# Expert matmuls in plain fp32 on four 32-column tiles of TensorE, without the hi/lo split of weights and activations

## The reference, cut to what matters

```python
def expert_choice_ffn(h, w_router, w_gate_up, w_down):
    B, N, D = h.shape
    cap = CAP_FACTOR * N // N_EXPERTS            # 64 sample tokens, 16 prompt tokens
    aff = jax.nn.softmax((h @ w_router).astype(jnp.float32), axis=-1)
    g, idx = lax.top_k(jnp.swapaxes(aff, 1, 2), cap)
    xs = jax.vmap(lambda hb, ib: hb[ib])(h, idx)
    gu = jnp.einsum('becd,edf->becf', xs, w_gate_up)      # 1024 -> 2 x 1024
    gate, up = jnp.split(gu, 2, axis=-1)
    y = jnp.einsum('becf,efd->becd', jax.nn.silu(gate) * up, w_down) * g[..., None]
    return jax.vmap(lambda ib, yb: jnp.zeros((N, D), yb.dtype).at[ib.reshape(-1)].add(yb.reshape(-1, D)))(idx, y)
```

## Time and profile before

| | us |
|---|---|
| median of 3 runs (927.48 to 930.04) | 929.23 |
| span of the profiled execution | 926.3 |
| expert matmuls, first start to the first matmul of the last stage | 350.5 to 901.4 |
| last stage | 901.4 to 926.3 |

### The profile page before, as it was taken

The page is one execution under the profiler, slowest core; times in us unless marked ns, Lnnn a source line. Parts: engine busy times, 40 slices in busy tenths (PEclk is TensorE's granted clock), DMA queues, the critical chain, the costliest instruction groups (busy, mean ns, idle before and its releaser), DMA issues.

```text
span 926.3 us, 12681 instructions
## 1 busy us (share of the span) xinstructions
PE 880.6 (95%) x5127; PEld 625.9 (68%) x5127; DVE 775.7 (84%) x828; ACT 583.5 (63%) x606; POOL 159.5 (17%) x109
## 2 busy tenths in 40 slices
PE   6989999698899979999999999999999999999995
PEld 5779977466688865666666666666666666666663
DVE  4579654889789877898998998898998998898877
ACT  2365376756622236777777777777777777777752
POOL 0000300010011052002312311321320320320220
PEclk9999999999999988999999999999999999999998
DMA  9920540450086479999999999999999999999717
GB/s 338 389 92 6 206 183 1 183 183 2 4 319 255 185 317 363 379 416 389 402 403 389 388 412 391 388 415 385 385 416 381 377 414 381 382 401 391 253 14 204
DMA packets 59349, 272.80 MB, mean 294 GB/s; under 512 B 6728, under 2 KB 7036, under 8 KB 42908
## 3 DMA queue, kind: packets, MB, share of 16 engines
q1 hardware_dynamic: 50848, 245.33, 67.3%
q0 software_dynamic: 7536, 24.00, 9.2%
q10 hardware_dynamic: 908, 2.68, 0.8%
HBM read 257.99 MB, written 14.00 MB: 294 GB/s over the span
## 4 chain that ended last, share of the span: by engine, by line
PE 81%; DVE 8%; ACT 5%; DMA 3%; issue 2%; SPq 1%; ACTq 0%; DVEq 0%
PE PS L998 23%; PE PS L999 23%; PE PS L1000 23%; PE PS L1213 2%; PE PS L1197 2%; DMA w_qkv<-in_w_in 2%; PE PS L1236 1%; PE PS L1375 1%; PE PS L1388 1%; PE PS L1167 1%; DMA acc_scratch<-ysc,idx_u 1%; ACT WX L726 1%; ACT xnT L669 1%; PE PS L1021 1%; PE PS L1289 1%
## 5 line engine op out<-in xcount | busy, mean ns | idle before, releaser
L1927 DVE TENSOR_TENSOR Wl<-wr,Wh 128x2048 fp32r<-128x2048 f32 x190 | 432.6, 2290 | 52.2 <-ACT Wh L912 52.1
L912 ACT ACTIVATE Wh<-wr 128x2048 fp32r<-128x2048 f32 x192 | 367.4, 1915 | 69.6 <-PE PS L1000 69.5
L998 PE MATMUL PS<-Wh,Xh 128*80 128x512 f32 x512 | 203.3, 397 | 1.3 <-ACT gate_act L934 0.8
L1000 PE MATMUL PS<-Wl,Xh 128*80 128x512 f32 x512 | 201.9, 394 | 0.0
L999 PE MATMUL PS<-Wh,Xl 128*80 128x512 f32 x512 | 201.7, 394 | 0.0
L564 POOL DMA_INDIRECT acc_scratch<-ysc,idx_u x15 | 81.2, 5412 | 418.5 <-DVE ysc L1958 418.5
L1000 PEld LDWEIGHTS PS<-Wl,Xh 128*80 128x80 f32 x512 | 76.1, 149 | 42.5 <-issue 0.7
L998 PEld LDWEIGHTS PS<-Wh,Xh 128*80 128x80 f32 x512 | 76.2, 149 | 42.1 <-issue 1.9
L999 PEld LDWEIGHTS PS<-Wh,Xl 128*80 128x80 f32 x512 | 76.2, 149 | 39.7 <-issue 0.7
L998 PE MATMUL PS<-Wh,HTh 128*80 128x512 f32 x256 | 101.6, 397 | 0.0
L999 PE MATMUL PS<-Wh,HTl 128*80 128x512 f32 x256 | 100.4, 392 | 0.0
(11 more groups left out here) (314 smaller groups left out, 1226.3 us busy)
## 6 DMA issues: line engine op xcount, KB each, us to landing
wr<-in_w_gate_up SPq DMA_DIRECT2D x128, 1024.0 KB, 12.2
wr<-in_w_down SPq DMA_DIRECT2D x64, 1024.0 KB, 11.0
ring<-in_w_mod SPq DMA_DIRECT2D x24, 1024.0 KB, 10.2
ring<-in_w_in SPq DMA_DIRECT2D x4, 1024.0 KB, 11.4
ring<-in_w_out SPq DMA_DIRECT2D x4, 1024.0 KB, 6.6
w_qkv<-in_w_in SPq DMA_DIRECT2D x4, 768.0 KB, 14.1
h_scratch<-h POOLq DMA_DIRECT2D x5, 512.0 KB, 5.5
acc_scratch<-xt POOLq DMA_DIRECT2D x5, 512.0 KB, 5.9
```

Of the source, the lines that this page charges most:

```text
L912: act.activation(Wh[n % NWH][:], wr[s][:], ACT.Copy).then_inc(W_hi, 1)
L998: pe.matmul(out, w[0], x[0], start=first, stop=False)
L1000: return pe.matmul(out, w[0], x[1], start=False, stop=last)
L1927: dve.tensor_tensor(Wl[s][:], wr[s][:], Wh[n % NWH][:].bitcast(F32), ALU.subtract).then_inc(W_lo, 1)
```

## The change

The expert matmuls take the weights as they land, in fp32, and the activations unsplit. The stationary operand is cut into 32 columns: the 64 sample columns make two tiles, the 16 prompt columns with 16 zeros one. In gate/up each slot has three groups of four matmuls of 512 columns: sample rows of gate (two row tiles by two column halves), sample rows of up, and prompt rows of all four quarters. A down slot has two groups for the samples and one for the prompt, in which the four tiles are two f blocks by two halves; the two f blocks are added on ScalarE and VectorE (`odd_half`, `y_prompt_rows`). So 12 matmuls per slot remain, in plain fp32, and results lie on 128 partitions. The split copies are gone, the space of `Wh` becomes three more slots (16 in all). `x_transposes` is one call after k = 3 and `h_transposes` one call two slots after the last gate/up slot; the latter transposes four 128x128 blocks of samples and four 48-row blocks of the prompt. GpSimd clears the padding columns instead of splitting two slots.

```diff
-NSLOT, NWH = 13, 4
+NSLOT, N_LOW = 16, 13
-X_AT, H_AT = (1, 4), (2, 3)
+X_AT, H_AT = 3, 2
@@ GpSimd
-        for n in range(W_POOL):
-            pool.wait_ge(W_hi, n + 1)
-            pool.tensor_tensor(Wl[n][:], wr[n][:], Wh[n][:].bitcast(F32), ALU.subtract).then_inc(W_lo, 1)
+        pool.wait_ge(lg_ps, CH)
+        for buf in (XT[0], XT[1], HT[0], HT[1]):
+            pool.memset(buf[:, :, SL:SLQ], 0.0).then_inc(zeroed, 1)
@@ ScalarE
+        def odd_half(e):
+            act.wait_ge(W_used, DN_END[e] + 1)
+            if e:
+                act.wait_ge(y_ok, e)
+            b = dn_banks(e)[1]
+            for a in range(2):
+                act.activation(y_odd[CAP_S:SL, H2 * a:H2 * a + H2], PS[64 + 32 * a:64 + 32 * a + CAP_P, 512 * b:512 * b + 512],
+                               ACT.Copy, scale=g_slot[CAP_S:SL, e:e + 1]).then_inc(odd_ok, 1)
...
-        act.activation(yh[0][:], ysc[0][:], ACT.Copy).then_inc(yh_ok, 1)
+        act.wait_ge(W_used, len(ORDER) - 4)
+        act.activation(yh[0][0:CAP_S, :], ysc[0][0:CAP_S, :], ACT.Copy).then_inc(yh_ok, 1)
         for h in range(2):
             act.wait_ge(y_ok, NE + h)
-            act.activation(yh[1][:, 512 * h:512 * h + 512], ysc[1][:, 512 * h:512 * h + 512], ACT.Copy).then_inc(yh_ok, 1)
+            act.activation(yh[1][0:CAP_S, H2 * h:H2 * h + H2], ysc[1][0:CAP_S, H2 * h:H2 * h + H2], ACT.Copy).then_inc(yh_ok, 1)
+        odd_half(NE - 1)
+        act.wait_ge(y_ok, NE + 2)
+        act.activation(yh[1][CAP_S:SL, :], ysc[1][CAP_S:SL, :], ACT.Copy).then_inc(yh_ok, 1)
@@ TensorE, gate/up slot
-                for q in range(4):
-                    cs = slice(512 * q, 512 * q + 512)
-                    last = three(bank(q, rows=SL), x, (Wh[hs][:, cs], Wl[s][:, cs]), k == 0, k == KC - 1)
+                for b, lo in ((GATE_B, 0), (UP_B, 1024)):
+                    for j in range(4):
+                        pe.matmul(PS[32 * j:32 * j + 32, 512 * b:512 * b + 512], x[:, 32 * (j % 2):32 * (j % 2) + 32],
+                                  w[:, lo + 512 * (j // 2):lo + 512 * (j // 2) + 512], start=(k == 0), stop=(k == KC - 1))
+                for j in range(4):
+                    last = pe.matmul(PS[32 * j:32 * j + 32, 512 * GU_P_B:512 * GU_P_B + 512], x[:, CAP_S:SLQ],
+                                     w[:, 512 * j:512 * j + 512], start=(k == 0), stop=(k == KC - 1))
@@ VectorE
+        def y_prompt_rows(e):
+            b = dn_banks(e)[1]
+            for a in range(2):
+                dve.wait_ge(odd_ok, 2 * e + a + 1)
+                last = dve.scalar_tensor_tensor(y_sum[CAP_S:SL, H2 * a:H2 * a + H2], PS[32 * a:32 * a + CAP_P, 512 * b:512 * b + 512],
+                                                g_slot[CAP_S:SL, e:e + 1], y_odd[CAP_S:SL, H2 * a:H2 * a + H2], ALU.mult, ALU.add)
+            link(last)
+            return dve.tensor_tensor(ysc[e % 2][CAP_S:SL, :], y_sum[CAP_S:SL, :], G2[CAP_S:SL, :], ALU.mult)
@@ y_evac
+            if e < NE - 1:
+                y_sample_half(e, 0)
+                y_sample_half(e, 1)
+                y_prompt_rows(e).then_inc(y_ok, 1)
@@ VectorE, last stage
         y_lo(1, 0, 0, H2)
         y_lo(1, 1, H2, D)
+        y_prompt_rows(NE - 1).then_inc(y_ok, 1)
+        dve.wait_ge(yh_ok, 4)
+        dve.tensor_tensor(yl[1][CAP_S:SL, :], ysc[1][CAP_S:SL, :], yh[1][CAP_S:SL, :].bitcast(F32), ALU.subtract).then_inc(yl_ok, 1)
         for c in range(FIN_ADD):
```

More of the change, by code:

```diff
@@ L100 @@
 OUT_ORDER = (PC,) + tuple(range(PC))
-W_POOL = 2
 N_HOLD = 8
@@ L903, in _, with x_copy @@
         act.activation(aff[:, 0:PC, :], aff[:, 0:PC, :], ACT.Exp).then_inc(lexp_ok, 1)
[L906 to L924, removed]
+        def x_copy(e):
+            act.wait_ge(x_t, 2 * e + 1)
+            act.activation(XT[e % 2][:, 0:4, 0:SL], x_bank(0).rearrange("p (k s) -> p k s", k=4), ACT.Copy).then_inc(xT_s[0], 1)
         def silu_gate(e):
@@ L948, in _ @@
+        x_copy(0)
+        for n in range(len(ORDER)):
             for e in range(NE):
[L949 to L952, removed]
+                if n == GU_END[e]:
                     silu_gate(e)
-                for h in range(2):
-                    if n == GU_END[e] + H_AT[h] + LEAD:
-                        h_split(e, h)
+                if e + 1 < NE and n == GU0[e] + X_AT:
+                    x_copy(e + 1)
+                if n == GU_END[e] + H_AT:
+                    hT_copy(e)
+                if n == DN_END[e] and e < NE - 1:
+                    odd_half(e)
@@ new lines, in _ @@
+                for j in range(4):
+                    last = pe.matmul(PS[32 * j:32 * j + 32, 512 * GU_P_B:512 * GU_P_B + 512], x[:, CAP_S:SLQ],
+                                     w[:, 512 * j:512 * j + 512], start=(k == 0), stop=(k == KC - 1))
+            else:
+                bs, bp = dn_banks(e)
+                if k == 0:
+                    pe.wait_ge(hTs_ok, e + 1)
+                    pe.wait_ge(hTp_ok, e + 1)
+                    if e and e < NE - 1:
+                        pe.wait_ge(y_ok, e)
+                for f in (2 * k, 2 * k + 1):
+                    lo = 1024 * (f % 2)
+                    for j in range(4):
+                        pe.matmul(PS[32 * j:32 * j + 32, 512 * bs:512 * bs + 512],
+                                  HT[e % 2][:, f, 32 * (j % 2):32 * (j % 2) + 32],
+                                  w[:, lo + 512 * (j // 2):lo + 512 * (j // 2) + 512], start=(f == 0), stop=(f == KC - 1))
+                for j in range(4):
+                    f, lo = 2 * k + j // 2, 1024 * (j // 2) + 512 * (j % 2)
+                    last = pe.matmul(PS[32 * j:32 * j + 32, 512 * bp:512 * bp + 512], HT[e % 2][:, f, CAP_S:SLQ],
+                                     w[:, lo:lo + 512], start=(k == 0), stop=(k == KC // 2 - 1))
@@ L1435, in _ @@
+            last.then_inc(W_used, 1)
+            if kind == "gu" and e + 1 < NE and k == X_AT:
+                x_transposes(e + 1)
+            for e_ in range(NE):
+                if n == GU_END[e_] + H_AT:
+                    h_transposes(e_)
         pe.wait_ge(y_ok, NE - 1)
```

259 lines of the change are left out of this document (120 added, 139 removed).

## The result

| | median us | lowest to highest | ratio to the kernel before, 95% interval |
|---|---|---|---|
| before, same chip | 929.63 | 927.48 to 931.61 (4 runs) | |
| after | 912.42 | 911.85 to 913.64 (4 runs) | 0.9823 [0.9802, 0.9843] |

17.2 us less, 1.8%, well outside the 0.3% that can be told from no change. The profiled execution of after took 912.27 us with a span of 910.5, against the span of 926.3 in the earlier trace rows: 15.8 us less.

The account below looks back on a forecast made before the run. TensorE was taken to bound the experts, 6 us behind the weights' floor. Its end 22.8 us earlier and a tail 4.0 us longer made -18.8, so 929.2 - 18.8 = 910.4 us; range 900 to 925.

Parts of the forecast that it names:

- one round of four tiles: Expert matmuls: four records, one per tile, take 0.43 us; 1152 rounds make 495.4 us.
- transposes and 31 changes of form: Experts on TensorE: transposes 23.3 us; 31 excursions from four tiles to the full array and back, 0.23 each, 7.1 us.
- first rounds at the lower clock: Start of the experts: TensorE's first matmuls run at the lower clock and cost 2.3 us more.
- wait before expert 1's gate and up: Not priced; the wait examined was `h_transposes` for silu and two products, some 2 us, with two slots, 5.2 us, for it.
- tail: After W, the last `W_used`: chunk 0's statistics start at W + 8.0 instead of W + 3.2; net +4.0 us, bounds +1 to +7.
- start of the stage: First expert matmul: stays where it was, since 8 slots lie ready and the first rows' copies end as early.
- Rival C: Expert matmuls: rounds do not overlap and are 0.592 us apart, +187 us, 1097; chance 0.06.
- rival D: Expert matmuls: the form does not hold the full clock; at 1.2 GHz +495 us, 1405; chance 0.04.
- the other bound, 37 us: Changes of form on TensorE: upper bound, 0.6 us, a whole record, each way; the lower bound was 0 if later ones hide.
- The weights' floor: Experts: the last weights land at about 870, plus one slot 873; TensorE was expected to end 6 us behind it.
- Rival A: Experts: the weights become the bound, stage end 873, 904.8 us, or 902 with the tail at +1; chance 0.10.
- Splits hidden: Experts: ScalarE and VectorE lose 367 and 433 us of splits, priced at nothing since they were not on the path.

Follow-up runs that it names:

- the second profile of before: The kernel before, unchanged, run and profiled once more: 929.86 us, ratio 0.9996, span 928.5, experts from 352.82 to 903.92.
- four variants: The changed kernel with 13 slots (911.15 us), without the prompt tail (907.98), with a new prompt tail (908.42), or with VectorE kept busy (913.08).
- with VectorE kept busy: Against the changed kernel, two extra VectorE products of 128x512 on a scratch tile in every slot: 913.08 us, ratio 0.9822.
- The two kernels with the waits per bank: The changed kernel with waits per bank before gate/up: 911.85 us; with the new prompt tail and chunk 0 loaded from ScalarE's queue as well: 906.28 us.
- the runs with less work: Against the changed kernel with 13 slots, the prompt group of four matmuls left out in all slots but the first of each matrix: 909.68 us, ratio 0.9793.
- the second profile of after: The changed kernel, unchanged, run and profiled once more: 912.31 us, ratio 0.9816, span 909.4, stage 351.80 to 880.56.
- the one without VectorE's last two: Against the changed kernel, expert 15's prompt product with G2 on GpSimd, its rows added by plain fp32 matmuls without `yh` and `yl`: 908.42 us, ratio 0.9777.

## Why the prediction was right

912.42 us against 910.4, within the range; the ledger in spans was -18.8 and came to -15.8, or -18.0 against the second profile of before (928.5 - 910.5), whose experts start as late as those of after. Term by term:

| term | predicted | measured |
|---|---|---|
| one round of four tiles | 0.43 us | 0.43 (slot 2.58) |
| transposes and 31 changes of form | 23.3 + 7.1 = 30.4 | 15 x 0.81 + 16 x 1.07 = 29.3 |
| first rounds at the lower clock | 2.3 | 4.07 - 2.57 = 1.5 |
| wait before expert 1's gate and up | none | 2.4 (before 0.9) |
| stage in all | 528.1 | 528.7, 528.8; in four variants 529.8 to 530.1 (before 550.9, 551.1) |
| tail | +4.0 | +3.9 (28.8 for 24.9) |
| start of the stage | 0 | +2.5 by this pair of profiles, +0.2 by the other |

That the stage comes out only 0.6 us off is luck in part: the missed wait of 2.4 us is set off by 1.1 too much for transposes and changes of form and 0.8 too much for the low clock.

**The round** was read from 256-column rows and doubled, and held for 1152 rounds. Rival C falls with it. The rule quoted there from the Trainium skill ("TensorE: Matmul & The Clock Gate", Part 3), 3.07x for four row tiles, is not what this form of four column tiles shows: untiled records are 0.429 apart and rounds of four 0.43, four for the price of one. Why the page's figure is lower can't be told from here, since row tiles were not run.

**The clock** (rival D) was granted in full, 1.00 from 385 to 880. After the wait before expert 1 it fell in five of the nine profiles of changed kernels that have this wait, though not in the two of after itself; the stage of the kernels with 13 slots, without the prompt tail and with VectorE kept busy was then 530.0 to 530.1 us. Why it fell in some and not in others stays open.

**The changes of form** were read from single gaps of 0.09 and 0.13 to 0.14; an added one costs 0.26 to 0.27. The word "hidden", 0 us, and the other bound, 37 us, are both far off.

**The wait at 378.43** is the step that failed. I looked for a wait at `h_transposes`, which has two slots of time; the silu of expert 0 is also what the gate and up banks of expert 1 wait for, and there the order of the slots puts no down products between. The other experts have them, and it costs once: 375.14 + 0.86 = 376.00, next matmul 378.43. It stood in a row of before, in the timeline and among the waits of that stage, which the prediction passed over with "waits for almost nothing":

```profile
376.51 0.43 PE L998 MATMUL PS<-Wh,Xh 128*80 128x512 f32 x1 [0.78 <-ACT gate_act L934]
```

With the interval of 0.23 before it, that is 0.9 us of idle time. The old kernel waited there bank by bank (`if e == 1 and k == 0`), and the change put one wait for all banks in its place. The two kernels with the waits per bank bring it back to 1.0.

**The weights' floor** I put at 873 and found at 877 (matmuls of the last stage at 876.7 when TensorE is no bound). In that execution the experts began at 352.26, 1.7 us later than in the earlier trace rows. And I took the median landing of the earlier trace rows, 5.1 us, for the last slot, where the longest was 7.3: in the first profile of before the DMAs still move 354 GB/s from 871 to 872 us and 23 in the next. The two make 3.9 us, against 3.7 missing (4.6 by the last slot's start). Rival A did not occur in after, but it is near: 1.5 us of full clock at the start and 1.4 from the bank waits were enough to make TensorE wait for weights. A faster TensorE would have gained some 4 us at most and, by the runs with less work and with the bank waits, little of it at the end, since chunk 1 of `xf` is used at 886.00 and 884.89 there and at 886.39 in after.

**The tail** went as worked out step by step: statistics at W + 8.1 for W + 8.0. That the scatter goes out at W - 3.7 and not at W - 5.8 is the load of chunk 0 behind the weights, landing later than my 872. This differs between executions: in the second profile of after it is W - 4.6, and with 13 slots and in the two kernels with the tail changed it waits for VectorE and goes out at W - 5.7, as predicted. In after it cost an idle 0.63 us on TensorE and nothing on VectorE's chain. The kernel without the prompt steps and the one without VectorE's last two give 4.3 and 3.9 us back, the whole term: it was VectorE's chain alone that set the end. I had doubted my own term there and was wrong to.

**Splits hidden.** VectorE gave up 351 us of work from 385 to 880 (449.35 there before, 97.99 after) and ScalarE 310 (364.43 and 54.13); the kernel without splits or tiles is 127 us slower. Freeing the two engines was worth nothing by itself, as TensorE sets the pace in all these kernels.

## What to carry to other kernels

Count TensorE's columns in the new form before counting what other engines save: a plain fp32 matmul of 512 columns is two records of 0.43 us, against 0.229 for an fp32r one and 0.69 for three of them; it pays here only because the short stationary operands leave room for four tiles, and only if successive matmuls go to different tiles. When the bounding stage is shortened, look at what is now just behind it, here a weight queue some 4 us away over the stage, and less at one point, and a load queued behind the weights, because it takes the next gain. Steps of few rows cost their columns, so in a tail that one engine sets, 16 rows are as dear as 80 and are worth moving to an idle engine even at twice the time.

## What the runs showed of the hardware

- Matmuls on four 32-column tiles issued tile after tile run 2.7 at a time over the stage, not one and not four (0.160 us per record against 0.107 in turn and 0.429 in order).
- 1.99 us of idle TensorE in the tail was followed by 5 us at 0.50 of the clock (1.2 GHz), and four matmuls took 3.78 us instead of 1.98; 0.63 us of idle time in the kernel after was not. The length of the idle time alone does not decide it: some 2.4 us before expert 1 were followed by a lower clock in five profiles (0.57 from 376 to 380 us with 13 slots) and by the full clock in four, the two of after among them.
- An excursion from 128x32 tiles to the full array and back costs 0.26 to 0.27 us.
- GpSimd's indirect scatter took 5.44 us to issue beside VectorE products of 2.29 us each, 1.44 without, and 1.74 beside products of 0.69 us.
